# Two transformer blocks on one core: where TensorE sums the norms' rows, and where two half low parts stand

## The reference

```python
h = rmsnorm(x, g_pre)                      # norm 0, 2 (first block), 4, 6 (second block)
merged = ...                               # projections, three branches, gates
x = x + rmsnorm(merged @ w_o, g_post)      # first block; the second adds merged @ w_out as it is
h = rmsnorm(x, g_ffn)                      # norm 1, 3 (first block), 5, 7 (second block)
x = x + rmsnorm(ffn(h) @ w_down, g_post)   # first block; the second adds ffn(h) @ w_down
```

## Time and profile before

| | |
|---|---|
| runs | 1871.13, 1884.57, 1887.86 us |
| the profiled execution | 1875.14 us |
| its span | 1873.3 us |
| mean granted TensorE clock | 0.989 of full speed |
| TensorE, VectorE, ScalarE busy | 97%, 73%, 58% |
| DMA queue of the stream | 582 loads of 512 KB, 50.5% of the 16 engines' time |

### The profile page before, as it was taken

The page is one execution under the profiler, slowest core; times in us unless marked ns, Lnnn a source line. Parts: engine busy times, 40 slices in busy tenths (PEclk is TensorE's granted clock), DMA queues, the critical chain, the costliest instruction groups (busy, mean ns, idle before and its releaser), DMA issues.

```text
span 1873.3 us, 36335 instructions
## 1 busy us (share of the span) xinstructions
PE 1811.1 (97%) x14784; PEld 1769.1 (94%) x14784; DVE 1363.1 (73%) x2385; ACT 1077.5 (58%) x1812; POOL 186.2 (10%) x200
## 2 busy tenths in 40 slices
PE   8999999999999999999999999999998998999998
PEld 8999999999999999999899889999998998899998
DVE  6997778867889779867767767655557687676553
ACT  5455656655455657654676775554456757745542
POOL 1012410001002410001111003000002100020000
PEclk9999999999999999999999999999998999999999
DMA  7545535563545535564536534565553364345552
GB/s 280 177 156 184 178 124 199 185 202 135 199 157 180 180 125 204 193 207 136 169 135 185 181 124 141 172 195 192 202 156 133 138 201 152 113 170 180 194 194 109
DMA packets 90342, 320.08 MB, mean 171 GB/s; under 512 B 10528, under 2 KB 12992, under 8 KB 90048
## 3 DMA queue, kind: packets, MB, share of 16 engines
q1 hardware_dynamic: 90176, 317.75, 50.5%
HBM read 310.60 MB, written 1.08 MB: 166 GB/s over the span
## 4 chain that ended last, share of the span: by engine, by line
PE 78%; DVE 11%; ACT 5%; issue 3%; POOL 1%; DMA 1%; SPq 0%; DVEq 0%; ACTq 0%; POOLq 0%
PE big L579 71%; PE small L579 5%; DVE L L1094 3%; PE small L578 2%; DVE POOL L1451 2%; ACT H L1871 1%; DVE POOL L1321 1%; DMA POOL<-POOL 1%; ACT POOL L2254 1%; POOL POOL L2465 1%; DVE POOL L1650 1%; DVE POOL L1283 0%; POOL POOL L2444 0%; ACT POOL L2291 0%; DVE gates L1338 0%
## 5 line engine op out<-in xcount | busy, mean ns | idle before, releaser
L579 PE MATMUL big<-HH,H 128*128 128x256 f32 x3344 | 952.1, 285 | 9.4 <-DVE gates L1338 5.7
L579 PE MATMUL big<-HL,H 128*128 128x256 f32 x3344 | 935.7, 280 | 3.9 <-DVE HL L1229 3.8
L579 PE MATMUL big<-HH,L 128*128 128x256 f32 x3344 | 934.8, 280 | 0.0
L1094 DVE TENSOR_TENSOR L<-F,H 128x1024 fp32r<-128x1024 f32 x574 | 701.9, 1231 | 202.3 <-ACT H L1871 201.3
L1871 ACT ACTIVATE H<-F 128x1024 fp32r<-128x1024 f32 x582 | 610.6, 1054 | 209.1 <-PE big L579 205.5
L579 PEld LDWEIGHTS big<-HH,H 128*128 128x128 f32 x3344 | 636.3, 190 | 14.8 <-DVE gates L1338 6.4
L579 PEld LDWEIGHTS big<-HL,H 128*128 128x128 f32 x3344 | 634.9, 190 | 7.7 <-DVE HL L1229 5.3
L579 PEld LDWEIGHTS big<-HH,L 128*128 128x128 f32 x3344 | 634.9, 190 | 0.0
L579 PE MATMUL big<-FH,H 128*128 128x256 f32 x848 | 240.0, 283 | 0.0
L579 PE MATMUL big<-FL,H 128*128 128x256 f32 x848 | 236.1, 278 | 0.0
L579 PE MATMUL big<-FH,L 128*128 128x256 f32 x848 | 236.1, 278 | 0.0
(11 more groups left out here) (239 smaller groups left out, 1812.8 us busy)
## 6 DMA issues: line engine op xcount, KB each, us to landing
F<-in_stream SPq DMA_DIRECT2D x582, 512.0 KB, 3.8
POOL<-POOL SPq DMA_DIRECT2D x32, 128.0 KB, 4.2
POOL<-head_rows SPq DMA_DIRECT2D x8, 256.0 KB, 5.0
X<-in_x SPq DMA_DIRECT2D x2, 512.0 KB, 4.4
POOL<-POOL SPq DMA_DIRECT2D x16, 64.0 KB, 2.8
out_x<-X SPq DMA_DIRECT2D x1, 1024.0 KB, 3.9
POOL<-in_decay SPq DMA_DIRECT2D x1, 768.0 KB, 11.1
POOL<-POOL SPq DMA_DIRECT2D x8, 96.0 KB, 5.0
```

The costliest lines, as they stand in the source:

```text
L579: return pe.e.matmul(out_, lhsT, rhs, start=start, stop=stop)
L1094: v.tensor_tensor(L[:, j % NR, :], F[:, j % NF, :], H[:, j % NR, :].bitcast(F32), ALU.subtract).then_inc(s_lo, 1)
```

## The change

TensorE's sums move. Before norms 1, 3, 5 and 7, row 6's set now follows the accumulated rows' set at the middle of `out` 7, and only row 7's set is left behind the group. Before norms 2, 4 and 6, the accumulated rows' set moves from behind `down` 7 to its middle; since it holds row 6, VectorE now takes an extra step of its staged tasks behind the first of a `down` group's low parts, so that row j - 1's product and addition stand there and no longer at the start of the next group. The two useless matmuls ahead of "s1" go at norms 1 to 4. The first two of the four half low parts of VectorE move from ahead of the small steps and ahead of the first row to behind rows 3 and 5.

```diff
-                keep_busy(3, 2 if b in SUMMED else 3)
+                keep_busy(3, 0 if b in SUMMED else 3)
...
-                if m.j == 7 or last_added(b) == 6:
+                if m.j == 7:
                     yield
                 if m.j == 6:
                     use(0, b, "yy")
...
                     sums_of(b, 0, True, False)
                     if last_added(b) == 6:
                         return
-                    yield
                 sums_of(b, m.j, False, m.j == 7)
...
                     plain_norm(b, layer, e, gain, l)
                     return
-                low_half()
                 bank, read = is_filled(b, "zx")
...
                 scaled(b, 1)
-                low_half()
                 for n in range(KT):
                     if n == KT - 1:
                         low_half()
...
                     if n % 2:
                         low_x(layer, e, n - 1)
-                        if n == KT - 1:
+                        if n > 1:
                             low_half()
...
                     if not full_banks(n):
                         low_parts(j + AHEAD)
+                    if j == rest[0] and g.members[0].label == "down" and g.members[0].j:
+                        staged.step()
```

## The result

The changed kernel takes **1899.66 us** (median of 8 runs, 1891.46 to 1902.54) against 1885.44 us for the kernel before on the same chip (8 runs, 1871.13 to 1890.76): the ratio is **1.0106, 95% interval 1.0077 to 1.0134**. Slower, and above the range's upper end of 1896. The profiled execution took 1902.54 us with a span of 1900.8 us.

The account below looks back on a forecast made before the run. TensorE, busy 97% of the span, was taken as the bound. Terms of -0.7, +1.3, +1.7, +1.9 and +0.8 gave +5.0 us on the four-run mean of 1879.7: 1884.7 us, range 1873 to 1896.

Parts of the forecast that it names:

- The waits at norms 2 and 4: Middle of down 7: TensorE stands waiting for VectorE's addition of row 6, 1.2 us at norm 2, 1.55 at norm 4.
- The clock falls in down 7: Second rival, chance 0.22: wait plus set in the dense group halve the clock, +6.8 us at two norms, 1891.5 us.
- Norm 2's closing stretch: Evidence against the second rival: behind norm 2's group the clock did not fall after 2.74 us of one-column instructions.
- The tail of norm 2, -1.2: Group's end to first row put out, at 2.4 GHz: shortened by 0.77 plus 0.42, together 1.2 us.
- The two halves, +0.2 a norm: Half low parts behind rows 3 and 5: TensorE waits 0.2 us at each of four norms, +0.8; bounds 0 and 5.0.
- Norms 1 and 3, -0.35 each: Out 7 and tail at the low clock: no wait, 8.1 to 8.2 us against 8.43, so -0.7 for both.
- Norms 5 to 7, +1.9: Sums moved into the last groups: +0.6 at norm 5, the same at 7, +0.7 at norm 6.
- Sum: All terms over the seven norms added up: +5.0 us for the profiled execution.
- The range: Whole kernel: 1873 us (fastest run plus third rival's +1.9) to 1896 us (slowest run plus sum and one fall).

Follow-up runs that it names:

- e4: The changed kernel measured and profiled once more, unchanged, on another chip: ratio 1.0083 to the kernel before.
- e12: The changed kernel with down 7's set of sums taken 8 blocks later and twice over: ratio 1.0112 to the kernel before.
- e11: The kernel before with TensorE only waiting for VectorE's addition in the middle of down groups, the set left in the tail: ratio 1.0011.
- e7: The changed kernel with TensorE's set of down 7 taken 8 blocks later, when the addition is done: ratio 1.0038 to the kernel before.
- e1: The kernel before with only the two half low parts moved behind rows 3 and 5 of norms 1 to 4: ratio 1.0009.
- e13: The changed kernel with TensorE's sums of norms 5, 6 and 7 back at their old places: ratio 1.0102 to the kernel before.

## Why the prediction was wrong, by its own steps

- **The waits at norms 2 and 4** (1.2 and 1.55 us) came out at 1.24 and 1.41 (1.24 and 1.52 in e4), the gaps in down 7 at 2.7 to 3.2 us against 2.5 and 2.85. Right, mechanism and size.
- **"The clock falls in down 7"** was the second rival, at 0.22, and is what happened; the sum put it at nothing. This is the step that failed first: the sum ran the blocks behind the wait at full clock, and the clock fell there nine times out of ten. Norm 2's closing stretch, which I held against it, has no idle wait ahead of its 24 one-column matmuls, and e12 shows that in down 7 such a stretch leaves the clock up to the group's end. The rows did not contradict the rival; they were of another case. The Trainium skill ("TensorE: Matmul & The Clock Gate", section "HAM oscillation — how this bites in real kernels") describes falls where matmuls wait for DMA between dense runs, in waits longer than these. The traces here show 0.50 of the clock behind a wait of 1.24 to 1.52 us with the set behind it, and 1.00 behind such a wait alone (e11). Its price: second part +1.9 us each (means 7.4 against 5.5), +3.7 for both norms; I had 3.4 for each, from falls of 6.8 us, and three of these four lasted 3.4. But in three of the four cases another came in the tail or over the rows, and that was in no term of mine.
- **The tail of norm 2, -1.2.** At norms 2 and 4 it is -0.6 on average (7.50 to 6.88), for "s2" runs at the low clock in three of the four (+0.52). Where the clock stays up the step was right: -1.1 (e7, 6.40, and e4 at norm 2, 6.41). The halves alone bought 0.9 of it at that clock (e1), and they cost 1.05 in the rows.
- **The two halves, +0.2 a norm.** They cost 1.05 (rows of 11.83 against 10.78 us at full clock and pace), five times the term, though under its bound of 1.24. Two mistakes: the half behind row 3 lasts 1.22 us beside GpSimd, and TensorE waits for row 6 as well as row 4. The hint was in reach: in the trace of before an addition of VectorE (L1205) beside GpSimd's takes 0.81 us instead of 0.42 (norm 4):

```profile
879.97 0.81 DVE L1205 TENSOR_TENSOR X<-X,POOL 128x256 f32<-128x256 f32 x1
```

```profile
879.77 0.73 POOL L2420 TENSOR_TENSOR X<-X,POOL 128x256 f32<-128x256 f32 x1
```

The Trainium skill ("SBUF — State Buffer", section "Who interferes with whom") says that the two engines share a pair of ports, an exclusive lock, and that a VectorE instruction with two inputs in SBUF contends with a GpSimd one that reads SBUF. The rows agree: the half took 0.55 us more than its 0.68 where 0.68 us of GpSimd's instruction were left, and GpSimd 0.52 more than its 0.74 where the half came first.
- **Norms 1 and 3, -0.35 each.** They cost +1.5 each, halves included. The gap grew by 1.5 as said (1.3 and 0.2 for the low clock), the rows took 1.05, and the tails gave back 1.1 us, where the working had 1.7 (8.43 to 6.7; its terms add up to -0.23 to -0.33, and it took -0.35).
- **Norms 5 to 7, +1.9.** Measured +2.1, and e13 takes it out. Right.
- **Sum.** +5.0 forecast, +16.3 measured at the norms. Of the 11.3 between them the clock within down 7 has 3.7, the rows 3.9 (4.7 for 0.8, one norm's partly at the low clock), the tails that gave back too little 2.8 (0.8 each at norms 1 and 3, 0.6 each at 2 and 4), the gaps in down 7 0.6; some tenths are spread over the rest.
- **The range.** It ended at the slowest run of four plus the sum and one fall. In the first profile both norms had a fall in down 7 and another behind it; I had let in one. The second measurement's median, 1893.61 us, lies inside the range, and that is luck: the kernel before took 1874.65 us beside it, so the difference was 19 us and not 5.

## What to carry to other kernels

Work moved out of a tail into a dense group must find its input ready: in down 7 an idle wait with one-column matmuls behind it brought the clock down for the blocks that follow, and the same work 8 blocks later did not. When several edits shorten one tail, price the whole set, for what each buys alone does not add up. And look at the clock before two tails are compared: 3.4 us less of low clock made an unedited tail 1.5 us shorter, more than any one edit bought at a like clock. Before VectorE gets another instruction, look at what GpSimd does in that moment, and give it the time in which VectorE waits, not the time in which it is next in line.

## Not expected of the hardware

- Two paces for the same 256-column matmuls at the same full clock, 342 or 355 to 356 of them in 40 us, held for up to 200 us and different in the same stage of another execution. Its cause is open; no edit here chose it.
- In down 7, one-column fp32 matmuls kept TensorE "busy" in the trace for 2.7 us and did not bring the clock down in the group (e12), nor did 1.3 to 1.5 us of idleness (e11); one after the other did. In out 7 such matmuls did it alone, after 2.3 us of them in the changed kernel at norm 1.
- A half low part of 0.68 us took 1.22 to 1.23 us behind row 3 at all four norms, beside GpSimd's HL (after, e1); behind row 5 it began first, kept its 0.68 us, and GpSimd's HL took 1.26 us in place of 0.74 (after, norm 4).
